# Down weights of 32 experts loaded in runs of 16 KB in place of 8 KB, with the activation written twice and turned in four blocks

## The reference, cut to what matters

```python
D_MODEL, SEQ, N_EXPERTS, D_EXPERT = 1024, 512, 32, 512

def hier_moe(h, ...):                       # top-1 group of 8 experts, top-2 experts in it
    t = h.reshape(-1, D)
    ...
    out = jnp.zeros_like(t)
    for e in range(N_EXPERTS):
        y = (jax.nn.silu(t @ w_gate[e]) * (t @ w_up[e])) @ w_down[e]
        out = out + combine[:, e:e + 1] * y
    return out.reshape(B_, L, D)
```

## Time and profile before

| | |
|---|---|
| runs before | 904.15, 904.58, 901.21 us (median 904.15) |
| span of the profiled execution | 900.3 us |
| the profiled execution's own time | not shown apart from its span; the three runs lie 0.9 to 4.3 us above the span |
| busy | TensorE 829.1 us (92%), VectorE 332.4 (37%), ScalarE 200.3 (22%), GpSimd 152.4 (17%) |
| DMA | 71,744 packets, 265.19 MB, mean 295 GB/s over the span |

### The profile page before, as it was taken

How to read it: one execution, slowest core, us unless ns; L and a number is a source line. 1 busy time by engine, 2 the same in 40 slices (tenths; PEclk the granted TensorE clock), 3 DMA queues, 4 the chain that set the end, 5 groups by cost and what they waited for, 6 DMA issues and landing times.

```text
span 900.3 us, 15459 instructions
## 1 busy us (share of the span) xinstructions
PE 829.1 (92%) x5319; PEld 572.9 (64%) x5320; DVE 332.4 (37%) x616; ACT 200.3 (22%) x295; POOL 152.4 (17%) x241
## 2 busy tenths in 40 slices
PE   7999999999999999998899899999989999997860
PEld 6888888888888888885555455555545555544430
DVE  4799996851464346348111011101111101110107
ACT  4633435131453214141000000000000000000003
POOL 4231801000130000010222112211212222111100
PEclk8999999999999999999999999999999999999995
DMA  8693330823333947668999999999999999999987
GB/s 250 142 196 100 95 94 14 181 74 115 94 94 140 384 177 259 243 222 311 384 417 422 420 422 423 422 425 422 423 422 426 423 421 428 419 425 423 425 333 274
DMA packets 71744, 265.19 MB, mean 295 GB/s; under 512 B 29526, under 2 KB 30550, under 8 KB 54516
## 3 DMA queue, kind: packets, MB, share of 16 engines
q1 hardware_dynamic: 65428, 254.10, 74.3%
q0 software_dynamic: 6128, 10.45, 3.1%
q10 hardware_dynamic: 144, 0.02, 0.0%
HBM read 256.59 MB, written 16.52 MB: 303 GB/s over the span
## 4 chain that ended last, share of the span: by engine, by line
PE 78%; SPq 7%; DMA 5%; DVE 5%; issue 2%; ACT 1%; POOL 0%; DVEq 0%; POOLq 0%; ACTq 0%
PE ps L1070 36%; PE ps L465 21%; PE ps L481 11%; DMA slot_x<-in_exp_w_gate 5%; SPq L448 4%; PE ps L1055 2%; SPq L446 2%; PE ps L471 1%; PE ps L1047 1%; DVE pair L709 1%; DVE pair L704 1%; DVE hl L754 1%; PE ps L1215 1%; PE ps L591 1%; PE ps L1181 1%
## 5 line engine op out<-in xcount | busy, mean ns | idle before, releaser
L704 DVE TENSOR_TENSOR pair<-pair,ps 128x256 f32<-128x256 f32 x32 | 13.5, 422 | 334.9 <-PE ps L465 334.9
L1497 DVE TENSOR_TENSOR w_lo<-raw,w_hi 128x1024 fp32r<-128x1024 f32 x56 | 73.5, 1313 | 99.7 <-ACT w_hi L1301 98.9
L1070 PE MATMUL ps<-h_hi,w_hi 128*128 128x512 f32 x280 | 109.2, 390 | 0.0
L1070 PE MATMUL ps<-h_hi,w_lo 128*128 128x512 f32 x280 | 109.0, 389 | 0.0
L1070 PE MATMUL ps<-h_lo,w_hi 128*128 128x512 f32 x280 | 108.9, 389 | 0.0
L1301 ACT CAST w_hi<-raw 128x1024 fp32r<-128x1024 f32 x59 | 61.8, 1050 | 189.4 <-PE ps L1070 189.4
L465 PE MATMUL ps<-ssm,pair 128*64 128x256 f32 x832 | 94.5, 384 | 4.9 <-DMA ssm<-in_exp_w_gate 4.2
L465 PEld LDWEIGHTS ps<-ssm,pair 128*64 128x64 f32 x832 | 61.1, 139 | 42.5 <-issue 15.2
L768 ACT COPY late<-ps 128x512 f32<-128x512 f32 x35 | 20.5, 586 | 299.6 <-PE ps L481 299.6
L852 POOL DMA_INDIRECT choice_rows<-late,put_now x35 | 35.5, 1015 | 292.3 <-ACT late L768 243.7
L1070 PEld LDWEIGHTS ps<-h_hi,w_hi 128*128 128x128 f32 x280 | 52.6, 188 | 11.0 <-issue 0.2
(11 more groups left out here) (341 smaller groups left out, 1215.6 us busy)
## 6 DMA issues: line engine op xcount, KB each, us to landing
ssm<-in_exp_w_gate SPq DMA_DIRECT2D x16, 2048.0 KB, 23.6
raw<-in_w_in SPq DMA_DIRECT2D x40, 512.0 KB, 4.0
au<-in_exp_w_up SPq DMA_DIRECT2D x8, 2048.0 KB
ssm<-in_exp_w_up SPq DMA_DIRECT2D x8, 2048.0 KB
ssm<-in_exp_w_down SPq DMA_DIRECT2D x8, 2048.0 KB, 22.8
hl<-in_exp_w_down SPq DMA_DIRECT2D x8, 2048.0 KB
slot_x<-in_exp_w_gate SPq DMA_DIRECT2D x8, 2048.0 KB, 30.5
raw<-in_exp_w_down SPq DMA_DIRECT2D x8, 2048.0 KB
```

The lines of the kernel that those rows point to most:

```text
L704: nc.vector.tensor_tensor(act_cols, silu_cols, up_now, ALU.mult).then_inc(act_ready, 1)
L1070: t = nc.tensor.matmul(bank, lhs, rhs, start=k == 0 and n == 0, stop=k == 2 * count - 1 and n == 2)
L1497: vv.tensor_tensor(w_lo[u % PAIRS][:], raw[:, u % RAW].rearrange("p (k n) -> p k n", k=2), w_hi[u % PAIRS][:], ALU.subtract).then_inc(w_lo ...
```

## The change

The down matrix is laid out as `(p j) n`: partition p holds the rows 4p to 4p + 3, one run of 16 KB. For the activation to match this, a turned column has to hold the hidden column 4p + j, where p runs over both halves of the hidden columns. The product on VectorE therefore writes each column group j twice side by side (128 columns: 64 tokens, and the same again), `turn_act` turns four blocks of 128x128 in place of two, and of each turned block the rows 0 to 63 are wanted for the lower half of the hidden columns and the rows 64 to 127 for the upper half. VectorE copies the one (64 partitions, 4 x 64 elements), ScalarE the other. `down` goes over j = 0 to 3 with the same number and size of matmuls, and waits for both copies. Set 3's down is still loaded by two DMAs, now the first and the second half of each partition's 16 KB. `act_` and `actT` change places in the tile `pair`, where `act_` is now 512 elements wide.

```diff
-        silu, act_ = pair[:, 1024:1280], pair[:, 1280:1536]
-        actT = pair[:, 1536:1792].rearrange("p (j n) -> p j n", j=2)
+        silu, act_ = pair[:, 1024:1280], pair[:, 1536:2048]
+        actT = pair[:, 1280:1536].rearrange("p (j n) -> p j n", j=KF)
...
-                 "down": exp_w_down[0].rearrange("e (h p j) n -> e p h (j n)", p=P, j=2)}
+                 "down": exp_w_down[0].rearrange("e (p j) n -> e p (j n)", p=P)}
...
-        at_bank = ps[:, B_AT, 0:256].rearrange("p (j n) -> p j n", j=2)
-        up_now, silu_cols = (a.rearrange("p (c j) -> p j c", j=2) for a in (ps[:, B_UP, 0:F // 2], silu))
-        act_cols = act_.rearrange("p (j c) -> p j c", j=2)
+        at_bank = ps[:, B_AT].rearrange("p (j n) -> p j n", j=KF)
+        up_now, silu_cols = (a.rearrange("p (c j) -> p j c", j=KF) for a in (ps[:, B_UP, 0:F // 2], silu))
+        act_twice = act_.rearrange("p (j two c) -> p j two c", j=KF, two=2)
...
             dst = slots[EW[w][kind]]
-            if kind == "down":
-                dst = slot_runs[EW[w][kind]]
-                if not isinstance(e, int):
-                    src = src.rearrange("e p h n -> p (e h) n")
-            elif not isinstance(e, int):
+            if not isinstance(e, int):
                 src = src.rearrange("e p n -> (e p) n")
             if w == SETS - 1 and kind != "gate":
-                if kind == "up":
-                    dst, src = slot_runs[EW[w][kind]], src.rearrange("p (h n) -> p h n", h=2)
+                dst, src = slot_runs[EW[w][kind]], src.rearrange("p (h n) -> p h n", h=2)
...
         def turn_act():
-            for j in range(2):
+            for j in range(KF):
                 t = nc.tensor.transpose(at_bank[:, j], act_[:, P * j:P * (j + 1)], ident[:])
             return t
+        def low_half(copy):
+            return copy(actT[0:CAP], at_bank[0:CAP, :, 0:CAP])
+        def high_half(copy):
+            return copy(actT[CAP:P], at_bank[CAP:P, :, CAP:P])
...
-            for n, (h, j) in enumerate((h, j) for h in range(2) for j in range(2)):
-                if n == 2 and pe is not None:
+            for j in range(KF):
+                if j == KF // 2 and pe is not None:
                     pe.wait_ge(rest_in["down"], rest)
                 for c in range(2):
-                    t = nc.tensor.matmul(ps[CAP * c:CAP * (c + 1), bank], actT[:, j, CAP * h:CAP * (h + 1)],
-                                         w[:, 2 * h + j, W * c:W * (c + 1)], start=n == 0, stop=n == 3)
+                    t = nc.tensor.matmul(ps[CAP * c:CAP * (c + 1), bank], actT[:, j], w[:, j, W * c:W * (c + 1)],
+                                         start=j == 0, stop=j == KF - 1)
+        def activated():
+            return nc.vector.tensor_tensor(act_twice, silu_cols.unsqueeze(2).to_broadcast((P, KF, 2, CAP)),
+                                           up_now.unsqueeze(2).to_broadcast((P, KF, 2, CAP)), ALU.mult)
...
-                pe.wait_ge(actT_ready, e + 1)
+                pe.wait_ge(actT_ready, e * 2 + 2)
...
-                nc.vector.tensor_tensor(act_cols, silu_cols, up_now, ALU.mult).then_inc(act_ready, 1)
+                activated().then_inc(act_ready, 1)
...
-                nc.vector.tensor_copy(actT, at_bank).then_inc(actT_ready, 1)
+                low_half(nc.vector.tensor_copy).then_inc(actT_ready, 1)
...
                 nc.scalar.activation(silu, ps[:, B_GATE, 0:HALF], ACT.Silu).then_inc(silu_ready, 1)
+                act.wait_ge(at_full, e + 1)
+                if not first:
+                    act.wait_ge(done["down"], e)
+                high_half(nc.scalar.copy).then_inc(actT_ready, 1)
```

More of the change, by code:

```diff
@@ L373, in trunk @@
         OV_XGT, OV_PRODUCT, OV_ACTT, OV_DVE = 1, 2, 3, 3
-        OV_SILU, OV_RES, OV_ACT = 1, 2, 2
+        OV_SILU, OV_ACTT_HIGH, OV_RES, OV_ACT = 1, 2, 3, 3
         def full(eng, name):
@@ L625, in experts_tensor @@
             banks_free(4, 7)
-            pe.wait_ge(actT_ready, 1)
+            pe.wait_ge(actT_ready, 2)
             pe.wait_ge(ew_in[0]["down"], 16)
@@ L665, in second_block @@
                     turn_act().then_inc(at2_full, 1)
-                    pe.wait_ge(actT2_ready, before + 1)
+                    pe.wait_ge(actT2_ready, before * 2 + 2)
                     pe.wait_ge(res2_ready, before + 1)
@@ L690, in over @@
                 pe.wait_ge(ov_dve, o_ * OV_DVE + OV_ACTT)
-                if not first:
-                    pe.wait_ge(ov_act, o_ * OV_ACT)
+                pe.wait_ge(ov_act, o_ * OV_ACT + OV_ACTT_HIGH)
                 down(0, B_RES[0]).then_inc(ov_pe, 1)
@@ L718, in turn @@
                     v.wait_ge(second_done, before * 3 + 3 + DONE["up"])
-                    nc.vector.tensor_tensor(act_cols, silu_cols, up_now, ALU.mult).then_inc(act2_ready, 1)
+                    activated().then_inc(act2_ready, 1)
                     v.wait_ge(at2_full, before + 1)
-                    nc.vector.tensor_copy(actT, at_bank).then_inc(actT2_ready, 1)
+                    low_half(nc.vector.tensor_copy).then_inc(actT2_ready, 1)
             turn(0, True)
@@ L733, in over @@
                 v.wait_ge(ov_pe, o_ * OV_PE + OV_UP)
-                nc.vector.tensor_tensor(act_cols, silu_cols, up_now, ALU.mult).then_inc(ov_dve, 1)
+                activated().then_inc(ov_dve, 1)
                 v.wait_ge(ov_pe, o_ * OV_PE + OV_AT)
@@ L737, in over @@
                     v.wait_ge(done["down"], NE)
-                nc.vector.tensor_copy(actT, at_bank).then_inc(ov_dve, 1)
+                low_half(nc.vector.tensor_copy).then_inc(ov_dve, 1)
             each_over(v, over)
@@ L781, in turn @@
                     nc.scalar.activation(silu, ps[:, B_GATE, 0:HALF], ACT.Silu).then_inc(silu2_ready, 1)
+                    act.wait_ge(at2_full, before + 1)
+                    high_half(nc.scalar.copy).then_inc(actT2_ready, 1)
                     results(res2, B_RES2, second_done, before * 3 + 3 + DONE["down"], res2_ready, second_rows, before * 16 + 16)
@@ L805, in over @@
                 nc.scalar.activation(silu, ps[:, B_GATE, 0:HALF], ACT.Silu).then_inc(ov_act, 1)
+                act.wait_ge(ov_pe, o_ * OV_PE + OV_AT)
+                if first:
+                    act.wait_ge(done["down"], NE)
+                high_half(nc.scalar.copy).then_inc(ov_act, 1)
                 if first:
```

## The result

The changed kernel takes 918.55 us in the median of four runs (917.36 to 919.44), the kernel before 903.81 in the four beside them. The ratio is 1.0165, with a 95% interval of 1.0149 to 1.0182. The forecast was 907.2 us and a range up to 911.5, so the measured time lies outside the range. Medians and ratios in this document leave out four single executions of 923 to 1461 us, in which the granted clock was 0.56 to 0.93 (one each of e2, e5, e7 and the kernel before). The profiled execution of the changed kernel took 918.16 us with a span of 916.4, 1.8 us more than the span. By this the profiled execution of before, with a span of 900.3, stood near 902.1 us, one of the shorter of its runs; this is why the spans differ by 16.1 us and the medians by 14.7.

What follows compares the result with a forecast made beforehand. Loads and TensorE were both nearly exhausted, with TensorE becoming the bound: 35 chains growing 0.50 us make 17.5 us, less 14.4 slack, so +3.1 on 904.15 gives 907.2 us. The range was 902.0 to 911.5.

Steps and rivals of the forecast that it cites:

- item 1 of the chain: VectorE's product between up and down: 512 elements per partition for 256, +0.26 us per chain, upper bound 0.27.
- the formula: End of the last down product: 35 chains times the growth per chain, less 14.4 us slack; forecast 3.1 us later.
- Transposes, +0.24: TensorE's turning of the activation before down: four transposes for two, +0.24 us per chain.
- Copies, 0: Copies before down: VectorE's unchanged at 425 ns, ScalarE's beside it at 372 ns, adding 0 to the chain.
- The rival of a late ScalarE: At down's wait for two copies: ScalarE's half ends late, each 0.1 us costing 3.5 us; 22%.
- Slack of 14.4 us, 35 chains: TensorE's spare time over the expert loop, 14.4 us, against 32 turns and 3 second blocks growing 0.50 us each.
- a tie at 0.37: End of the loop: with chain growth under 0.37 us the loads still pace, 902.7 us; rival, 17%.
- TensorE becomes the bound, waits for weights vanish: End of the expert loop: DMA waits disappear and TensorE runs 4.4 us behind the loads.
- Loads, -2.3 us: Down's weight loads in the expert loop: 16 KB packets for 8 KB save 2.3 us of DMA time.
- The two windows of 6 us: DMA stretches of mostly 8 KB and 16 KB packets, 416 and 425 GB/s, on which the 2.3 us rested.
- The clock: TensorE's clock in the chain's stretch without matmuls, 2.0 us for 1.5: rival that it falls, 955 us; 3%.
- The direction: Whole kernel against a 0.5% threshold: same 0.62, slower 0.34, faster 0.04.

Runs made afterwards that it cites:

- e2: Kernel before with only the loads of down in 16 KB runs (24 of 32), chain unchanged, so down multiplies wrong rows; ratio 0.9988 to the kernel before.
- e5: Changed kernel with ScalarE's silu reading PSUM every 4th element and writing side by side, so VectorE strides by 4 only in PSUM; 906.36 us, ratio 1.0027.
- e7: Changed kernel with silu turned by ScalarE, product written once, eight small matmuls against identity halves for four transposes, one VectorE copy; ratio 0.9990.
- e1: Changed kernel with eight forms of VectorE's product added behind the last expert to time each by itself; 918.72 us (one execution).
- form 5: One of the eight products added in e1: 512 elements by repeating, silu (SBUF) read side by side, up (PSUM) every 4th element; 0.69 us.
- e6: As e5, but the product writes each column group once (256 elements), so the upper half of hidden columns holds old values; 901.06 us, ratio 0.9973.
- e3: Changed kernel with down's loads put back to 8 KB runs, so down multiplies wrong rows; 920.09 us, ratio 1.0170 to the kernel before.
- e8: As e7, but the turned activation lies in two PSUM banks, VectorE copying two of its four blocks and ScalarE the other two; ratio 0.9996.

## Why the prediction was wrong

**The step that failed is item 1 of the chain, the product at +0.26 us.** It was taken from L486, a product of the same size, also out of PSUM and with a repeated operand. L486 reads its large operand in PSUM, and writes side by side into SBUF; it has no step of 4 elements on the side of SBUF. The change's product reads silu in SBUF so. The text even named the step ("for which no row has a price") and then set the upper bound at 0.27, the maximum of the same instruction: that is no bound for an unknown. Measured: +0.64, and 35 x 0.38 = 13.3 us of the result are this one term. With it alone put right the formula gives 35 x 0.88 - 14.4 = +16.4 in place of +3.1; with the whole chain as measured (0.85) it gives +15.4; the profile shows +16.4, of which 1.0 came in at the start of the loop. e5, where only this term goes back to 0.27, comes out at +0.27% for the +0.34% forecast.

A page of the Trainium skill bears on it that the prediction did not weigh. The Trainium skill (SBUF — State Buffer, "Door 1: The DMA port swizzle") describes lines of 16 bytes in SBUF: full bandwidth needs at least two accesses to a line, each access that crosses to a new one is paid, and how far one can stride for free is put at 4 float32. The forms of e1 agree with the lines: steps of 1 and 2, with two elements or more in a line, run at the same speed, and a step of 4, with one, takes 1.05 us for 0.69. If that figure of the Trainium skill is read as a step of 4 that is still free, the measurement speaks against it. The same section of the Trainium skill gives PSUM lines of 8 bytes and warns that strides there slow matmuls; VectorE's read of PSUM with a step of 4 cost nothing (form 5), nor did ScalarE's (383 ns for silu in e5, 385 before).

**What held.**
- *Transposes, +0.24*: 0.22. Two more cost less than the pair of L455 rows suggested, by 0.02.
- *Copies, 0*: right. VectorE's takes 417 ns on 64 partitions, ScalarE's 368, and both start together; TensorE waits for VectorE's. The rival of a late ScalarE falls.
- *Slack of 14.4 us, 35 chains*: e6 hides some 7 us, e7 ends in a tie at 0.26 per chain, and e5 to the whole change gives 12.5 us for 13.0 by the sum. That e7 is a tie already at 0.26 and not at 0.37 comes from the start of the loop, which the sum had taken as fixed: by the starts of the down products e7's long turns there exceed a free one by 7.3 us for 4.3 before, and its first down product is 0.8 us later than the chain explains. These 3.8 us eat slack like added work. The forecast of a tie at 0.37 was too generous by that.
- *TensorE becomes the bound, waits for weights vanish*: right, in both the profile after and e3.
- *Loads, -2.3 us*: right in sign, probably too large. e2, the one run that changes the loads alone, puts it at 1.1 us (0 to 2.1), four kernels together near 1.2; e6 by itself allows 2.3. The two windows of 6 us, on which the 2% rested, were thin, as the text said, and they differ in more than the long packets: 40 of the 347 packets in the earlier trace rows are under 512 B, and 18 of the 175 in the stretch of the earlier trace rows, by the DMA views of the two stretches.
- *The clock*: 1.00 in all of the loop after its start; the dip near 815 us is gone, and so is the idle time of 3 us before it. A chain of 2.3 us without a large matmul did not lower it. The Trainium skill (TensorE: Matmul & The Clock Gate, "Part 4: PE-mode transpose") says that a transpose does not count as busy in the same way; four of them in each chain in place of two left the clock of the loop at 1.00.

**The range** failed for the same reason. It covered ScalarE's lateness up to 0.12 us per chain; the term that carried the unknown had been closed at its upper end by the row of another instruction. The direction was forecast as within 0.5% with 62%, slower with 34%. Since every 0.1 us in the chain is 3.5 us, the unpriced step alone should have moved weight to the slower side.

## What to carry to other kernels

When two resources are both nearly exhausted, sum up the slack of the second before taking load off the first: here a gain of about a microsecond on the loads was bought with work in a chain that repeats 35 times, and what is bought only counts while the slack lasts. A price from another instruction holds for its access pattern, not for its size alone: compare the step of each operand, and on which memory. If an order has to be changed, let it happen in PSUM's reads (or in an engine off the chain, as silu is), and keep the SBUF side of VectorE at a step of 1 or 2 float32. (In PSUM only VectorE's second operand and ScalarE's input were tried with a step of 4, and in SBUF only VectorE's first operand; its result was tried with a step of 128.)

## What the runs showed of the hardware

- VectorE, float32, two operands, 512 elements: 0.69 us with SBUF steps of 1 or 2 elements, 1.05 us with a step of 4 on the read, 1.03 with a scattered write; 256 elements: 0.42 and 0.60. Reading PSUM with a step of 4 adds nothing, and neither does a repeated operand.
- ScalarE reads PSUM with a step of 4 in the time of one (383 and 385 ns for 256 elements).
- Eight float32 matmuls of 64 columns against 64 columns of the identity (16 records) take 0.69 us, as much as four transposes of 128x128 (0.66), and can put two halves of a tile on different partitions.
- TensorE pauses for which the profile names no releaser stand before gate and up products of the experts 2 to 8, ahead of the hardware loop and in its first two rounds: 2.4 us in all in the kernel before, 2.8 in the changed one, 3.5 in e7 and 4.3 in e8. Small changes of the program move them to other turns. The traces point at the loading of instructions: in before, after, e2, e6, e7 and e8 there are 15 of these pauses, and 2.3 to 3.7 us before the end of each a packet of 16 KB begins in the DMA queue of the kind "instruction" (before: between 498.0 and 498.5 us, for the pause that ends at 500.77). From 540 to 860 us the kernels before and after have no such packet and no such pause. Some of these packets pass without a pause, and no run changed them, so this is a coincidence in time and not a cause shown. The DMA view of before, 498 to 501 us:

```profile
q8 instruction: 1, 0.02, 2.2%
```

- The kernel before varies by some 4 us from run to run (901.22 to 905.68 in 17 runs), and versions bound by TensorE vary as much: e3 by 4.0 us in four runs (916.66 to 920.68), e5 by 5.1 in eleven (903.67 to 908.78); the changed kernel's four lie within 2.1 (917.36 to 919.44).
